# Weight-stationary expert loop: VectorE takes the first pair of up tiles before, not after, the split of one weight piece

## The reference

```
top_logit, top_e = top_k(x @ w_router, 2)          # 8 experts, 2 for each token
for an expert e and its rows xb:
    y = (silu(xb @ w1[e]) * (xb @ w3[e])) @ w2[e]   # 1024 -> 3584 -> 1024
```

## Time and profile before

| what | value |
|---|---|
| median of three runs | 2046.12 us (2045.82 to 2048.55) |
| the profiled execution | 2042.14 us |
| its span, first to last instruction | 2040.5 us |
| mean granted clock of TensorE | 0.996 |
| TensorE busy | 98% of the span |
| VectorE busy | 77% of the span |
| ScalarE busy | 54% of the span |
| chain that ended last | TensorE 86%, VectorE 9% |

### The profile page before, as it was taken

One profiled execution on the slowest core, in us unless ns is written; L12 is line 12 of the kernel. 1 busy time (PEld: TensorE's weight loads), 2 busy tenths in 40 slices (PEclk: granted clock), 3 DMA queues, 4 the chain that ended last, 5 costly groups with the idle time before them and its releaser, 6 DMA issues.

```text
span 2040.5 us, 34437 instructions
## 1 busy us (share of the span) xinstructions
PE 1990.0 (98%) x12290; PEld 1761.5 (86%) x12291; DVE 1570.0 (77%) x1978; ACT 1101.6 (54%) x1273; POOL 116.5 (6%) x104
## 2 busy tenths in 40 slices
PE   7999999999999999999999999999999999999997
PEld 6889787878779788999999988888999888999875
DVE  6866535353557585888888899999888898888998
ACT  6532423232335423555655577777655777555775
POOL 0000000000000000300100010100100100000250
PEclk9999999999999999999999999999999999999999
DMA  5312723232322123877787799999877899877993
GB/s 198 105 61 93 269 82 103 82 103 82 106 79 83 62 73 131 247 267 260 240 279 247 248 343 379 352 390 362 282 264 258 290 384 353 280 255 247 332 410 130
DMA packets 218751, 449.50 MB, mean 220 GB/s; under 512 B 13264, under 2 KB 64480, under 8 KB 218704
## 3 DMA queue, kind: packets, MB, share of 16 engines
q1 hardware_dynamic: 210560, 421.05, 59.1%
q0 software_dynamic: 8144, 27.82, 3.6%
HBM read 431.87 MB, written 16.96 MB: 220 GB/s over the span
## 4 chain that ended last, share of the span: by engine, by line
PE 86%; DVE 9%; issue 2%; ACT 2%; DMA 0%; DVEq 0%; ACTq 0%; SPq 0%; POOLq 0%
PE ps L617 17%; PE ps L619 17%; PE ps L618 17%; PE ps L959 15%; PE ps L976 8%; PE ps L961 6%; PE ps L978 3%; DVE w_lo L1845 1%; PE ps L686 1%; DVE w_lo L1848 1%; DVE w_lo L1401 1%; PE ps L641 1%; DVE ex L1426 1%; ACT w_hi L1251 0%; PE ps L880 0%
## 5 line engine op out<-in xcount | busy, mean ns | idle before, releaser
L959 PE MATMUL ps<-xt,w_hi 128*128 128x304 f32 x1792 | 457.2, 345 | 2.9 <-issue 2.9
L1845 DVE TENSOR_TENSOR w_lo<-raw,w_hi 128x1024 fp32r<-128x1024 f32 x336 | 409.3, 1218 | 55.3 <-ACT w_hi L1251 52.2
L1251 ACT ACTIVATE w_hi<-raw 128x1024 fp32r<-128x1024 f32 x340 | 357.7, 1052 | 123.5 <-PE ps L961 73.3
L961 PE MATMUL ps<-xt,w_lo 128*128 128x152 f32 x1792 | 420.0, 234 | 0.0
L1848 DVE TENSOR_TENSOR w_lo<-raw,w_hi 128x1024 fp32r<-128x1024 f32 x336 | 408.8, 1217 | 0.0
L1253 ACT ACTIVATE w_hi<-raw 128x1024 fp32r<-128x1024 f32 x340 | 356.5, 1049 | 1.1 <-DMA raw<-in_moe_w_dram 1.1
L961 PEld LDWEIGHTS ps<-xt,w_lo 128*128 128x128 f32 x1792 | 342.9, 191 | 0.1
L959 PEld LDWEIGHTS ps<-xt,w_hi 128*128 128x128 f32 x1792 | 338.8, 189 | 3.5 <-issue 3.4
L617 PE MATMUL ps<-act_hi,w_hi 128*128 128x512 f32 x608 | 242.1, 398 | 5.2 <-DVE act_lo L1446 5.2
L619 PE MATMUL ps<-act_hi,w_lo 128*128 128x512 f32 x608 | 239.9, 395 | 0.0
L618 PE MATMUL ps<-act_lo,w_hi 128*128 128x512 f32 x608 | 239.8, 394 | 0.0
(11 more groups left out here) (362 smaller groups left out, 3222.6 us busy)
## 6 DMA issues: line engine op xcount, KB each, us to landing
raw<-in_moe_w_dram SPq DMA_DIRECT2D x672, 512.0 KB, 5.4
raw<-in_w_in_dram SPq DMA_DIRECT2D x19, 1024.0 KB, 5.1
raw<-in_ffn_w_gate_dram SPq DMA_DIRECT2D x11, 1024.0 KB, 5.3
raw<-in_ffn_w_up_dram SPq DMA_DIRECT2D x11, 1024.0 KB, 5.3
raw<-in_ffn_w_down_dram SPq DMA_DIRECT2D x11, 1024.0 KB, 4.9
raw<-in_w_out_dram SPq DMA_DIRECT2D x8, 1024.0 KB, 4.9
y_rows<-mult POOLq DMA_DIRECT2D x1, 8192.0 KB, 28.9
y_rows<-yacc POOLq DMA_DIRECT2D x7, 512.0 KB, 5.2
```

Source lines behind the costliest of these rows:

```text
L959: pe.matmul(pairs_of(ps[:, bank, 0:2 * NW]), hi_[:, k % 4, f * P:(f + 1) * P], xt[:, k, :, 0:NW], start=k == 0, stop=False)
L961: last = pe.matmul(ps[:, bank, NW:2 * NW], lo_[:, k % 4, f * P:(f + 1) * P], xt[:, k, 0, 0:NW], start=False, stop=k == KT - 1)
L1251: act.activation(slot_hi[p % 6][:, 0:half], raw6(p)[:, 0:half], ACT.Copy).then_inc(w_hi_half, 1)
L1845: dve.tensor_tensor(slot_lo[p % 6][:, 0:half], raw6(p)[:, 0:half], f32(slot_hi[p % 6][:, 0:half]), ALU.subtract)
```

## The change

In the turned loop, and in its written-out twin for a last item, `rest_ahead(10, at_)` is moved from in front of the wait for `up_ps` and `hidden_turned(q + 1, 0)` to behind them. VectorE's order becomes gate 1, wait for `up_ps`, hidden 0, splits of pieces 10 and 11, wait for `w_used`, hidden 1. Nothing is added or taken away, and no other engine's program changes.

```diff
--- before.py
+++ after.py
@@ -2083,9 +2083,9 @@
                     gate_turned(q + 1, 0)
                     rest_ahead(9, at_)
                     gate_turned(q + 1, 1)
-                    rest_ahead(10, at_)
                     dve.wait_ge(up_ps, q + 2)
                     hidden_turned(q + 1, 0)
+                    rest_ahead(10, at_)
                     rest_ahead(11, at_)
                     dve.wait_ge(w_used, at_ + (MOE0 + 8))
                     hidden_turned(q + 1, 1)
```

## The result

| | before | changed |
|---|---|---|
| median | 2046.88 us (4 runs) | 2071.01 us (2070.47 to 2072.25, 4 runs) |
| ratio | | 1.0117, 95% interval 1.0105 to 1.0129 |
| profiled execution, span | 2042.14, 2040.5 us | 2070.47, 2068.8 us |
| mean granted clock | 0.996 | 0.992 |

What follows compares the result with a forecast made beforehand. The turned loop was taken as bound by TensorE without any gap; 23 iterations losing 1.00 us each gave 23.0 us, added to 2046.1 for 2069.1 us, range 2063 to 2075.

Steps and rivals of the forecast that it cites:

- Step 1: VectorE's first hidden step, put ahead of piece 10's split, already starts on TensorE's signal: gain 0, nearly 3 us idle.
- Steps 2 and 3: On VectorE, splits of pieces 10 and 11 follow the first hidden step; the second hidden step starts 1.84 us late.
- Step 4: TensorE's down tile d = 2 waits for banks 6 and 7: 0.94 us late, 1.00 us lost with the restart.
- Step 5: VectorE's third add still ends 0.6 us before TensorE's next gate needs it; nothing adds up or is recovered between iterations.
- Step 6: Queues: SyncE's loads wait 3.7 and 2.3 us longer for the splits; ScalarE and the matmuls are not held; counted nothing.
- The first item's first iteration, change 0: Both TensorE waits already cost there; the first, 0.38 us, turns into a longer second; the second pair's signal stays: 0.
- its own last sentence: Prediction wrong if line 976 does not wait, waits much over 1 us, or an adds wait or lower clock shows.
- the third rival: TensorE's clock falls in the new pauses: 0.57 us a stretch, 13 us in 23 iterations, 2082 us or more; chance 4%.

Runs made afterwards that it cites:

- the second session: The changed kernel measured once more, nothing altered, against the kernel before: 2066.46 us against 2046.27, ratio 1.0106.

## Why the prediction was right

I forecast 2069.1 us, 23.0 over the kernel before, in 2063 to 2075; measured were 2071.0 and 24.1 (20 in the second session). Point by point:

- *Step 1, no gain from the earlier first hidden step:* right. VectorE idles 2.90 us there and TensorE never waited for it. What the idle time then costs depends on where the splits go: with piece 11's behind the second hidden step it still cost 19 us, and with piece 12's behind the third add as well the loop ran as before.
- *Steps 2 and 3:* right to the hundredth: 5.89 us between the hidden steps.
- *Step 4, the price:* late by 0.93 where 0.94 was worked out, but 0.96 to an iteration rather than 1.00. Five iterations went from 121.33 to 126.15 us. In the mean of these five the pause costs 0.92, the next pair 0.06 more (0.316 instead of 0.252), and the other down pairs 0.04 more; the 32 pairs of the gate take 8.04 us instead of 8.11 and give 0.07 back. Why the gate's pairs are shorter no run shows. 22.2 us for 23 iterations, not 23.0.
- *Step 5, the third add's cover:* right; 0.7 us are left of it, and when that was used up in an experiment the wait came at line 959.
- *Step 6, queues:* right, by the kernels in which the splits are later still and the loop runs as before.
- *The first item's first iteration, change 0:* **the step that failed.** The signal's time and the longer second wait were right (1.90 us, "about 2"). What I did not price is what was measured behind this one pause: a granted clock of 0.50 and pairs of 0.46 us for some 3.4 us, 1.5 to 1.6 us lost, in both profiled executions of the changed kernel (behind 1.90 and 1.83 us of idle time), where the kernel before has 1.30 us at this place and a clock of 1.00 behind it. The clock was a rival, but priced for the 23 short pauses of 0.76 us, and it stayed at 1.00 behind all of them; the loss came with the one long pause. By its own last sentence (wrong if "a lower clock shows") the prediction was wrong here. That the sum still came within 1.1 us of the measured 24.1 is in part luck: two errors, -0.8 for the 23 iterations and +1.6 for the first, stand against each other.
- *The price of a low stretch, in the third rival:* too small. It was taken from a window of 1.7 us, 0.57 us lost, but that stretch ran on from 828.4 to 831.8 in the kernel before, and the stretches of that length in the traces here cost 1.3 to 1.7 us each, by their pairs. By that the rival's own time would have been 2069 + 23 x 1.5, about 2104 us, and not 2082.

What the runs leave open is why the time outside the loop differs by some us from one execution to the next. No kernel here beats the one before by more than its measurement can tell: its loop has no gap in the steady iterations, and what the order that took away the first item's 1.85 us of waiting gained, it paid back at the items' ends.

## What to carry to other kernels

When an engine's instruction is moved ahead, ask first what it waits for: a step that already starts on its producer's signal can't start earlier, and the work that stood in front of it was filling the wait (here the step had started 0.04 us behind TensorE's last matmul, and moving it ahead left VectorE idle for 2.90 us). Then follow that work to the next signal that the bounding engine needs, and compare the chain with the cover there: here 6.80 us against 5.86, paid in full in every iteration. Read from the trace which pauses the clock held through, and price what is longer as open: in the expert stages of the ten traces here the pauses of 0.76 to 1.49 us of idle time were followed by a clock of 1.00, and 34 of the 42 pauses of 1.79 to 2.94 us by one of 0.50, most of them at 1.3 to 1.7 us lost.

## What the runs showed of the hardware

In these runs the cost of a pause had a step in it. Pauses of TensorE in the middle of a steady loop, at 25 to 29 us from one to the next: 0.93 us, a granted clock of 1.00 behind all 23; 1.52 us, 1.00 behind all 23; 2.05 us, a clock of 0.50 and pairs of 0.46 instead of 0.25 us behind 17 of 23, mostly some 7 pairs (3.4 us, 1.5 us lost) and in three of them some 13. The other pauses fit in. By idle time (0.76, 1.35 and 1.89 us for those three) single ones of 1.28, 1.30 and 1.49 us were followed by a clock of 1.00, those of 1.79 to 1.82 us at the items' ends by one of 0.50 in three of four, and 1.83, 1.90, 1.94, 2.51 and 2.94 us in the first item each time. No pause of the expert stage here lies between 1.49 and 1.79 us. Length alone does not decide it: 6 of the 23 at 1.89 us, and one of 2.53 us in front of the first matmul of the experts where nine of 2.48 to 2.53 did, were not followed by a low clock. In the changed kernel 0.60 us of VectorE work added to each iteration cost 14.2 us of waiting, which is 0.59 in each of 24; 1.14 us added cost 27.0 us of waiting, 1.13 in each, and some 28 us more at the low clock. The same 1.14 us in the kernel before cost 4 us in all.
